# Feature-major matmuls of one width in runs of 32 instead of 16, in a two-layer fp32 decoder trunk

## The reference

```python
q, k, v = split(h @ w_qkv)                     # 2048 x 6144: q and k are the first 32 units
x = x + attention(q, k, v) @ w_o
q = (h @ w_q).reshape(b, s, 8, 2, 128)         # PEER query: 16 units per layer
s1 = einsum('bshd,hkd->bshk', q[..., 0, :], keys_1)
s2 = einsum('bshd,hkd->bshk', q[..., 1, :], keys_2)
ids, g = top16_of_pairs(top16(s1), top16(s2))  # and a softmax over the 16
act = gelu(einsum('ced,cd->ce', expert_u[ids], h))
x = x + einsum('ce,ced->cd', g * act, expert_v[ids])
```

## Time and profile before

| what | value |
| --- | --- |
| median of 3 runs | 3718.28 us (3715.74 to 3719.6) |
| profiled execution | 3719.29 us, of it span of the core 3717.5 us |
| TensorE busy | 3682.6 us, 99% |
| L1484, high matmuls | 5120 |
| L1487, low matmuls | 5120 |
| granted TensorE clock | 0.998 of full speed on average |
| longest TensorE wait | 9.5 us, once, for the first high half |
| TensorE waits for low activations (L969) | 2.9 us in 4, longest 1.4 |

### The profile page before, as it was taken

How to read it: one execution, slowest core, us unless ns; L and a number is a source line. 1 busy time by engine, 2 the same in 40 slices (tenths; PEclk the granted TensorE clock), 3 DMA queues, 4 the chain that set the end, 5 groups by cost and what they waited for, 6 DMA issues and landing times.

```text
span 3717.5 us, 47415 instructions
## 1 busy us (share of the span) xinstructions
PE 3682.6 (99%) x19152; PEld 3160.6 (85%) x19152; DVE 2130.3 (57%) x3020; ACT 1666.2 (45%) x2016; POOL 1538.6 (41%) x833
## 2 busy tenths in 40 slices
PE   8999999999999999999999999999999999999998
PEld 7888888888888888888878888888888888888887
DVE  5555689666666544444456548976666654444444
ACT  4355444444444444444445543444444444444444
POOL 2211466787882122222212136678888412222221
PEclk9999999999999999999999999999999999999999
DMA  9844557998777767766644355578777676666664
GB/s 351 273 156 154 188 199 244 260 260 246 209 214 233 253 235 244 243 241 238 246 173 171 113 193 182 204 215 215 212 215 210 210 265 239 240 247 239 237 248 171
DMA packets 255435, 825.54 MB, mean 222 GB/s; under 512 B 88816, under 2 KB 154352, under 8 KB 171760
## 3 DMA queue, kind: packets, MB, share of 16 engines
q1 hardware_dynamic: 128832, 718.38, 55.3%
q10 hardware_dynamic: 52656, 103.82, 7.9%
q0 software_dynamic: 73728, 0.29, 4.2%
HBM read 752.94 MB, written 69.47 MB: 221 GB/s over the span
## 4 chain that ended last, share of the span: by engine, by line
PE 94%; DVE 4%; ACT 1%; issue 0%; DMA 0%; DVEq 0%; SPq 0%; ACTq 0%
PE bank L1484 29%; PE bank L1487 15%; PE bank L1641 12%; PE bank L1645 12%; PE bank L1643 12%; PE bank L1507 3%; PE bank L1509 3%; PE bank L1508 3%; DVE match L1125 1%; DVE lo L897 1%; DVE bank L914 0%; PE bank L1600 0%; DVE sel_f L1135 0%; PE bank L1581 0%; PE bank L1582 0%
## 5 line engine op out<-in xcount | busy, mean ns | idle before, releaser
L897 DVE TENSOR_TENSOR lo<-raw,hi 128x1024 fp32r<-128x1024 f32 x975 | 1208.9, 1241 | 1355.9 <-ACT hi L548 1354.6
L548 ACT ACTIVATE hi<-raw 128x1024 fp32r<-128x1024 f32 x1278 | 1348.4, 1058 | 1314.8 <-PE bank L1645 699.7
L498 POOL TENSOR_TENSOR lo<-raw,hi 128x1024 fp32r<-128x1024 f32 x303 | 736.7, 2433 | 1959.3 <-ACT hi L548 1959.3
L1484 PE MATMUL bank<-act_t,hi 128*128 128x512 f32 x5120 | 1227.8, 392 | 14.6 <-ACT hi L548 9.5
L1484 PEld LDWEIGHTS bank<-act_t,hi 128*128 128x128 f32 x5120 | 942.1, 189 | 201.0 <-issue 9.5
L515 POOL DMA_INDIRECT w_rows<-gate,place_u x512 | 797.3, 1557 | 195.1 <-issue 151.3
L1487 PEld LDWEIGHTS bank<-act_t,lo 128*128 128x128 f32 x5120 | 659.7, 191 | 29.2 <-DVE act_t L969 3.7
L1487 PE MATMUL bank<-act_t,lo 128*128 128x256 f32 x5120 | 675.1, 283 | 3.1 <-DVE act_t L969 2.9
L1641 PE MATMUL bank<-hi,wa 128*128 128x512 f32 x2040 | 628.1, 389 | 0.9 <-DVE stage L916 0.9
L1645 PE MATMUL bank<-hi,wa 128*128 128x512 f32 x2040 | 628.0, 389 | 0.0
L1643 PE MATMUL bank<-lo,wa 128*128 128x512 f32 x2040 | 628.0, 389 | 0.0
(11 more groups left out here) (236 smaller groups left out, 1876.0 us busy)
## 6 DMA issues: line engine op xcount, KB each, us to landing
raw<-in_stream SPq DMA_DIRECT2D x647, 1024.0 KB, 4.9
w_rows<-zeros SPq DMA_DIRECT2D x64, 512.0 KB, 8.4
act_rows<-stage ACTq DMA_DIRECT2D x64, 512.0 KB, 3.7
acts<-act_rows ACTq DMA_DIRECT2D x64, 512.0 KB, 4.3
w_part<-w_rows ACTq DMA_DIRECT2D x64, 512.0 KB, 5.5
w_rows<-gate,place_u POOLq DMA_INDIRECT x512, 4.5
xt_in<-in_x_t SPq DMA_DIRECT2D x4, 512.0 KB, 7.8
x_res<-in_x SPq DMA_DIRECT2D x2, 1024.0 KB, 14.3
```

The costliest lines, as they stand in the source:

```text
L498: pool.tensor_tensor(lo[:, s, :], raw[:, n0 % RAW_SLOTS, j * HALF:(j + 1) * HALF], hi[:, s, :].bitcast(F32), ALU.subtract).then_inc(lo_rea ...
L548: act.activation(hi[:, s, :], half, ACT.Copy).then_inc(hi_ready[s], 1)
L897: dve.tensor_tensor(lo[:, s, :], half, hi[:, s, :].bitcast(F32), ALU.subtract).then_inc(lo_ready[s], 1)
L1484: ins = mm(ps[:], hi[:, s, at], act_t[:, kt, :, :].rearrange("p w t -> p (w t)"), start=(kt == 0), stop=(kt == KT - 1), skip_group_check=True)
```

## The change

Only TensorE's program changes, in `unit_a`. All units without `rows` go through a new function: all 16 high matmuls and then all 16 low ones in units of even number, low first in odd ones. `middle` stands between the two runs. A slot is released in the second run, after its 8 matmuls there. The first matmul of a unit starts the accumulation, be it high or low.

```diff
+            def whole_unit(n0, ps, middle=None):
+                slots = [(s, k) for _, s, k in halves(n0)]
+                high_first = n0 % 2 == 0
+                for run, high in enumerate((high_first, not high_first)):
+                    for j, (s, k) in enumerate(slots):
+                        pe.wait_ge((hi_ready if high else lo_ready)[s], k + 1)
+                        for q in range(KT // 2):
+                            kt = KT // 2 * j + q
+                            at = slice(q * P, (q + 1) * P)
+                            first, last = run == 0 and kt == 0, run == 1 and kt == KT - 1
+                            if high:
+                                ins = mm(ps[:], hi[:, s, at], act_t[:, kt, :, :].rearrange("p w t -> p (w t)"),
+                                         start=first, stop=last, skip_group_check=True)
+                            else:
+                                ins = mm(ps[:, 0:S], lo[:, s, at], act_t[:, kt, 0, :], start=first, stop=last,
+                                         skip_group_check=True)
+                        if run == 1:
+                            ins.then_inc(used[s], 1)
+                    if run == 0 and middle:
+                        middle()
+
             def unit_a(n0, idx, middle=None, rows=None):
                 pe.wait_ge(a_free, idx + 1)
-                weights_by_features(n0, ps_a[idx % 2], middle, rows)
+                if rows is None:
+                    whole_unit(n0, ps_a[idx % 2], middle)
+                else:
+                    weights_by_features(n0, ps_a[idx % 2], middle, rows)
```

## The result

| | median us | ratio to before, 95% interval |
| --- | --- | --- |
| before | 3718.56 (3715.74 to 3719.6) | 1 |
| changed | 3787.94 (3786.47 to 3788.21) | 1.0185 [1.0173, 1.0198] |

The forecast was 3716.2 us. The profiled span grew from 3717.5 to 3786.0 us. The page of the changed kernel, beside the earlier trace rows: busy time and counts by engine, the chain by engine, and GpSimd's indirect DMAs (busy us, mean ns | idle before).

What follows compares the result with a forecast made beforehand. TensorE's matmul gaps plus 35 us of standstill were taken as the bound. Profiled 3719.3 us, less 3.1 for seams, plus 1.0 for stalls, gave 3717.2, or 3716.2 us as median; range 3711.5 to 3722.5.

Steps and rivals of the forecast that it cites:

- Spacing and seams: TensorE's matmul stream: each period with two width changes costs 20 ns extra; 157 fewer periods save 3.1 us.
- (a): TensorE's seams: the 20 ns are not tied to width changes, no gain, 3719.3 us; chance 0.14 together with (d).
- (d): TensorE's matmul gaps depend on columns alone: seams cost nothing, stalls stay, as (a); chance 0.14 together with (a).
- Later releases ... hidden, cost zero: Long stretch: later-freed weight halves push ScalarE and VectorE by 0.1 to 0.2 us; 1.8 of 2.0 us slack left.
- 0.96 and 1.81: First weight half: now freed 0.96 us before an even unit's end, 1.81 us before an odd one's.
- If that slack were gone, every unit would pay: Long stretch: caveat on the slack of 2.0 us before TensorE wants VectorE's summed bank, 1.8 of it left.
- worst case, +7: Routing stretches: stalls of 2.2, 0.8 and 2.2 us reach the end, plus 1.6 us of half clock, about +7.
- Rival (c): End-of-routing stretches: VectorE and GpSimd hinder each other, nine odd units stall 2.2 us each, 3735 us; chance 0.08.
- The stall of unit 95: First layer's end of routing: TensorE waits 2.2 us for GpSimd's low half, 1.2 of it reaching unit 97.
- +0.8: First layer's end of routing: VectorE starts 0.8 us later, with no idle time to recover it.
- half clock: TensorE after a standstill, in the worst bound: 8 wide gaps of 0.2 us more, 1.6 us.

Runs made afterwards that it cites:

- e12: Changed kernel with its new order only in the PEER queries and first 22 expert_u units of both layers, old order elsewhere: 3722.09 us, 1.001 of before.
- e6: Changed kernel with the low run first in every unit, so runs of 16 and equally late releases everywhere: 3717.14 us, 0.9994 of before.

## Why the prediction was wrong

**Spacing and seams: right.** 27 ns per change of width independent of the run's length, 11.113 us for two units against 11.114. Rivals (a) and (d) fall with it.

**"Later releases ... hidden, cost zero": the step that failed.** I followed the later release through ScalarE and VectorE to the bank, found 1.8 us of slack, and was right about those: TensorE never waits in the long stretch. I left out GpSimd, whose preparations a low half of VectorE can hold. They are a chain of 497 us in the first layer with a deadline at its end, and they depend not on how late VectorE's work is but on whether it comes at the same place in each unit. I had the 0.85 us of alternation in my own lines (0.96 and 1.81) and did not ask who else times itself by it. The terms I put at zero: an 88 us longer scatter less 48.5 us of margin, which is 39.0 us of waiting on TensorE, and 25.1 in layer 2. "If that slack were gone, every unit would pay" named the wrong slack.

**The bounds.** My worst case, +7, rested on the two routing stretches; I bounded no term in the longest stretch because no one waited there. Rival (c) had the right pair of engines, VectorE and GpSimd, and the right sign, but the place (routing), the operation (low halves on GpSimd) and the mechanism were others.

**The stall of unit 95: size right, neighbours wrong.** Waits in unit 95, beside the earlier trace rows:

```profile
595.12 1.18 PE L1506 MATMUL bank<-act_t,lo 128*128 128x256 f32 x8 [1.53 <-POOL lo L498]
598.31 1.62 PE L1506 MATMUL bank<-act_t,lo 128*128 128x256 f32 x8 [2.01 <-POOL lo L498]
```

The second low half waits 2.01 us (forecast 2.2), but the first one waits 1.53 us as well, and the granted clock in that stretch fell to 0.97 on average (1.00 before). The windows, beside the earlier trace rows:

```profile
583.00:640.00 57.00, 53.08 (x287) 45.87 (x287) 47.39 (x57) 25.76 (x32) 35.34 (x15) 0.97 0.72 233
2366.00:2430.00 64.00, 63.31 (x376) 56.15 (x375) 59.04 (x149) 29.79 (x37) 41.35 (x17) 1.00 0.58 203
1249.00:1255.00 6.00, 5.56 (x23) 5.15 (x24) 4.54 (x6) 2.73 (x4) 0.00 (x0) 0.56 0.70 249
```

At 583:640 TensorE now idles 3.9 us (2.6 before), and VectorE is busy only 47.4 of 57 (54.5): it was not as full as I took it to be. Busy time of VectorE can be time held by GpSimd, as the 9.20 us for four L1125 in the earlier trace rows suggest (the same four took 1.42 us in four other units of the stretch and up to 5.07 in the rest); how much of it was, no run separates. At 2366:2430 TensorE idles 0.7 (1.4 before). e12 prices both stretches at 3.4 us, where I had +0.8 less 0.7 for seams. The last matmul of each unit, read in both traces, says where: between units 84 and 103 the changed kernel falls back by 4.5 us (forecast +0.8), and between 391 and 415 it wins 1.4 (forecast 0). About 2.9 of the 4.5 are lost by unit 92, ahead of the window that I had looked at; waits for L916 of 0.68 us at 539.8 and 1.14 at 576.0 stand there, where before there was one, of 0.27, at 579.5. That term was too small, and its place in part wrong. The last row shows a granted clock of 0.56 behind the long standstill, near the lower of the two levels, 1.2 GHz; it adds to the two waits, as the prediction allowed for shorter ones.

**A small miss.** Unit 6 waits for the inverse in its middle, where it did not wait before:

```profile
51.93 0.68 PE L1581 MATMUL bank<-inv_diag,ones 128*128 128x128 f32 x4 [0.37 <-DVE inv_diag L937]
```

**The sum.** 3719.3 - 3.1 + 39.0 + 25.1 = 3780.3 of the profiled execution's 3787.8 us. The ends of the units give most of the other 7.5. Unit 204 ends 3.2 us later than before and unit 205 44.6: the first standstill costs 41.4 us, 2.4 more than its wait. Units 515 and 516 end 40.6 and 68.3 us later, which is 27.8 us for a wait of 25.1. So the half clock behind the two waits costs about 5 us (I had 1.6 for one), and the two routing stretches 3.1. That makes 3788.4; what is left is within what two executions differ by.

## What to carry to other kernels

When a change alters when buffers come free, follow it to every engine that shares a port or a queue with those it moves, not only to those that wait for the buffers, and look up the deadline of each long chain in the background: the scatter had 48.5 us to spare, which was in the trace. A background stream whose period nearly divides the loop's may owe its speed to the loop's regularity; a change that makes neighbouring iterations unlike breaks that, so keep releases at the same place in each, or measure the stream's pace with the alternation alone.

## What the runs showed of the hardware

A preparation of an indirect DMA takes 1.55 us on GpSimd, with 0.3 us to the next. If it starts within about 1.0 us after VectorE has begun a 1.23 us subtraction of two SBUF operands, it ends 1.42 us after that subtraction instead (180 of 512 in the changed kernel); if it starts 0.3 to 0.5 us ahead of it, as in the kernel before and in e6, neither is slowed. A change from 256 to 512 columns costs TensorE 27 ns spread over five matmuls, whether 8, 16, 32 or 120 narrow ones went before; one from 512 to 256 gives 7 back. Behind standstills of 39.0 and 25.1 us the granted clock was 0.56 over the next 6 us, which cost about 2.5 us each time.
